# Up projection of an encoder layer: seven block products in place of eight

## The chip, the cores and the metric

The kernel runs on one core of a Trainium2 chip. The metric is the device time of one execution in microseconds (us). Three runs of the kernel before took 3253.85, 3255.36 and 3263.27 us; the median is 3255.36. TensorE is called PE here, VectorE DVE, ScalarE ACT, GpSimd POOL; SP is the engine that issues most DMAs.

## The reference, cut to what matters

One layer of a bidirectional encoder, 2048 tokens of 1024 channels in float32: an input projection, RWKV-7 time mixing beside windowed attention, an output projection with residual, and then a ConvGLU. The change lies in the ConvGLU's up projection, 1024 x 5632:

```python
x = x + jnp.concatenate([y_rwkv, y_attn], axis=-1) @ w_out[l]
x = x + conv_glu(rms_norm(x, g_ffn[l]), w_up[l], conv_w[l], conv_b[l], w_down[l])

def conv_glu(h, w_up, conv_w, conv_b, w_down):
    T = h.shape[1]
    u = h @ w_up                                  # (2048, 1024) @ (1024, 2 * 2816)
    up = jnp.pad(u, ((0, 0), (1, 1), (0, 0)))
    u = sum(up[:, i:i + T] * conv_w[i] for i in range(3)) + conv_b
    g, val = jnp.split(u, 2, axis=-1)
    return (jax.nn.silu(g) * val) @ w_down
```

## The kernel before, in words

The program is a row of stages, each a block of five instruction streams (one per engine) that meet only at semaphores: first, attention, rwkv_project, gates, recurrence, mix, up, down. All tensors lie with 128 channels on the partitions and tokens along the free dimension. A float32 product is made of three matmuls (`product`, L88 to L93): both operands are split into a high part (rounded to fp32r) and a low part (what is left), and high x high, high x low and low x high are summed in PSUM. The high half of a split is a copy on ACT (L2137, L1821 and others), the low half a subtraction on DVE (L2191, L1929).

**Mix** (`mix_block`, L1591) makes x + concat @ w_out in 32 slots, 4 quarters of 512 tokens by 8 tiles of 128 channels, in three PSUM banks in turn. A slot is 24 matmuls on PE, the addition on DVE (L1965), a square on ACT (L1843), a sum on POOL (L1901), and a store to `x2_dram` by SP (L1724). After each quarter PE sums the squares over the channels (L1781), ACT takes the root (L1847) and DVE the reciprocal (L1975), which gives the factor `inv_all` of the norm. While the last quarter runs, mix reads back the first two quarters (L1701), scales them on POOL and DVE (L1890, L1970), splits them, and splits the first two weight tiles; at its end PE already makes two products of the next stage (`up_ahead`).

**Up** (`up_block`, L2011) takes 22 pairs j. A pair is a gate tile and a value tile of 128 output channels each, over all 2048 tokens: 2 tiles x 4 quarters x 8 blocks of depth x 3 matmuls = 192 matmuls. Each quarter has a PSUM bank of its own (8 in all). The split tokens stay in SBUF for the whole stage. ACT copies each finished quarter to `up_raw` (L2148), DVE makes the depthwise convolution from it over 2048 tokens (one tensor_scalar L2210, two scalar_tensor_tensor L2213, L2216), ACT takes the sigmoid (L2154, into the memory of `inv_all`), DVE multiplies twice (L2221, L2226), SP stores (L2065). The weights of the next tiles are loaded into one buffer (L2052) and split. Pairs 1 to 20 are a loop; pair 0 and pair 21 are written out. The order on each engine is the order in which the code is written; no scheduler moves anything.

**Down** (`down_block`, L2256) reads the stored products back, and starts when all engines have left the up stage (`end_phase`, L416).

## Time and profile before

| what | us |
|---|---|
| median of three runs | 3255.36 (3253.85 to 3263.27) |
| profiled execution, span from first to last instruction | 3261.5 |
| mean granted clock of PE over the span | 0.963 |
| PE busy | 2993.0 (92%) |
| DVE busy | 1565.6 (48%) |
| ACT busy | 1039.5 (32%) |
| POOL busy | 770.6 (24%) |
| first matmul of the up projection, last one | 1782.8, 2756.6 |
| first matmul of the down projection | 2775.9 |

The profiled execution is one of its own; its time is known by its span only, which lies between the middle and the slowest of the three runs. The up projection is the longest stage, 974 of 3261 us. A row for a group of instructions gives their number, their busy time, the mean duration of one, and then the idle time of the engine just before them with what ended it. Matmuls overlap in the records: one lasts about 390 ns and the next begins some 227 ns after it began, so the busy share of PE says only that it did not stop. The granted clock is 1.00 at 2.4 GHz and 0.50 at 1.2 GHz.

### The profile page before, as it was taken

How to read it: one execution, taken by the hardware profiler on the slowest of the kernel's cores; microseconds unless marked ns; L12 is line 12 of the kernel's file. 1: busy time of each engine (PE TensorE's matmuls, PEld its weight loads, DVE VectorE, ACT ScalarE, POOL GpSimd, SP SyncE). 2: the span in 40 equal slices, each digit the busy share in tenths (PEclk: the TensorE clock that was granted, in tenths of full speed). 3: DMA queues.
4: the chain of work that ended last, by engine and by line, in shares of the span. 5: the costliest groups of instructions: out<-in, count | busy, mean ns of one | idle time of the engine just before them, and what ended most of it. 6: DMA issues, size and time to landing. Idle time of an engine off the chain costs nothing. (4 is left out here: it accounts for less than half of the span.)

```text
span 3261.5 us, 63594 instructions
## 1 busy us (share of the span) xinstructions
PE 2993.0 (92%) x26436; PEld 2417.1 (74%) x26436; DVE 1565.6 (48%) x2033; ACT 1039.5 (32%) x2012; POOL 770.6 (24%) x874
## 2 busy tenths in 40 slices
PE   7879989997658999996999899999999998999999
PEld 4554578884358999994667788888888886788887
DVE  4556723336665555634446644443444444333333
ACT  4436711114434444433244311111111111222222
POOL 4436700005436777631333300000000000000000
PEclk9998999998869999998999999999999999999999
DMA  3331223224883333224653211111111111631330
GB/s 116 136 91 43 53 78 71 65 52 131 306 248 98 115 118 116 85 91 144 205 168 134 82 49 51 46 38 51 51 51 46 50 51 41 241 100 47 100 100 35
DMA packets 236276, 317.60 MB, mean 97 GB/s; under 512 B 81593, under 2 KB 164025, under 8 KB 233234
## 3 DMA queue, kind: packets, MB, share of 16 engines
q1 hardware_dynamic: 231154, 308.99, 29.6%
q10 hardware_dynamic: 4896, 5.38, 0.5%
q8 instruction: 168, 2.75, 0.4%
q14 instruction: 58, 0.48, 0.1%
HBM read 211.17 MB, written 103.14 MB: 96 GB/s over the span
## 5 line engine op out<-in xcount | busy, mean ns | idle before, releaser
L91 PE MATMUL up_p<-h_hi,up_w_hi 128*128 128x512 f32 x1408 | 550.4, 391 | 10.1 <-DVEq L2187 3.9
L93 PE MATMUL up_p<-h_hi,up_w_lo 128*128 128x512 f32 x1408 | 549.5, 390 | 0.0
L92 PE MATMUL up_p<-h_lo,up_w_hi 128*128 128x512 f32 x1408 | 549.3, 390 | 0.0
L2148 ACT COPY up_raw<-up_p 128x512 f32<-128x512 f32 x176 | 103.3, 588 | 755.9 <-PE up_p L93 749.4
L91 PEld LDWEIGHTS up_p<-h_hi,up_w_hi 128*128 128x128 f32 x1408 | 265.4, 188 | 66.5 <-issue 7.3
L92 PEld LDWEIGHTS up_p<-h_lo,up_w_hi 128*128 128x128 f32 x1408 | 265.4, 189 | 55.6 <-issue 0.2
L93 PEld LDWEIGHTS up_p<-h_hi,up_w_lo 128*128 128x128 f32 x1408 | 265.2, 188 | 55.3
L2210 DVE TENSOR_SCALAR up_con<-up_raw,vecs_sb 128x2048 f32<-128x2048 f32 (+2 forms) x45 | 59.6, 1324 | 500.1 <-ACT up_raw L2148 500.1
L91 PE MATMUL down_p<-down_act_hi,down_w_hi 128*128 128x512 f32 x704 | 275.0, 391 | 18.9 <-DVE down_act_lo L2364 18.9
L92 PE MATMUL down_p<-down_act_lo,down_w_hi 128*128 128x512 f32 x704 | 274.9, 390 | 0.0
L93 PE MATMUL down_p<-down_act_hi,down_w_lo 128*128 128x512 f32 x704 | 274.7, 390 | 0.0
L2361 DVE TENSOR_TENSOR down_w_lo<-down_w,down_w_hi 128x1024 fp32r<-128x1024 f32 x88 | 107.8, 1225 | 308.9 <-ACT down_w_hi L2343 308.9
L2343 ACT CAST down_w_hi<-down_w 128x1024 fp32r<-128x1024 f32 x88 | 92.4, 1050 | 352.1 <-PE down_p L93 336.0
L91 PEld LDWEIGHTS down_p<-down_act_hi,down_w_hi 128*128 128x128 f32 x704 | 132.8, 189 | 47.0 <-issue 19.4
L93 PEld LDWEIGHTS down_p<-down_act_hi,down_w_lo 128*128 128x128 f32 x704 | 132.7, 189 | 27.8
L92 PEld LDWEIGHTS down_p<-down_act_lo,down_w_hi 128*128 128x128 f32 x704 | 132.7, 189 | 27.5
L561 POOL TENSOR_SCALAR attention_prob<-attention_prob,attention_inv 128x384 f32<-128x384 f32 (+1 forms) x96 | 117.1, 1236 | 59.7 <-DVE attention_inv L628 59.7
L1157 POOL TENSOR_TENSOR rec_V<-rec_V,rec_part 128x31 f32<-128x31 f32 (+15 forms) x217 | 123.1, 567 | 17.0
L91 PE MATMUL mix_p_out<-mix_hi,mix_w_hi 128*128 128x512 f32 x256 | 110.9, 433 | 13.7 <-DVE mix_lo L1929 13.7
L1153 POOL TENSOR_TENSOR rec_part<-rec_W,rec_V 128x31 f32<-128x31 f32 (+15 forms) x217 | 118.0, 544 | 22.4 <-issue 6.2
L91 PE MATMUL first_p_proj<-h_hi,first_w_hi 128*128 128x512 f32 x192 | 85.2, 444 | 35.5 <-POOL first_w_lo L357 23.7
L742 ACT COPY rwkv_project_raw_pad<-p_rwkv 128x512 f32<-128x512 f32 x56 | 32.9, 588 | 255.3 <-PE p_rwkv L93 255.3
(255 smaller groups left out, 6421.4 us busy)
## 6 DMA issues: line engine op xcount, KB each, us to landing
rec_inp<-gate_chunks SPq DMA_DIRECT2D x64, 512.0 KB, 3.6
down_act<-act_out SPq DMA_DIRECT2D x88, 256.0 KB, 2.8
up_w<-in_w_up SPq DMA_DIRECT2D x42, 512.0 KB, 4.0
act_out<-up_con SPq DMA_DIRECT2D x21, 1024.0 KB, 4.2
first_w<-in_w_attn SPq DMA_DIRECT2D x24, 512.0 KB, 4.6
rkv_chunks<-rwkv_project_mix SPq DMA_DIRECT2D x12, 1024.0 KB, 6.5
gate_chunks<-gates_out SPq DMA_DIRECT2D x3, 4096.0 KB, 11.7
down_w<-in_w_down SPq DMA_DIRECT2D x22, 512.0 KB, 12.8
```

The costliest lines, as they stand in the source:

```text
L91: pe.matmul(out, w_hi, x_hi, start=start, stop=False)
L92: pe.matmul(out, w_hi, x_lo, start=False, stop=False)
L93: return pe.matmul(out, w_lo, x_hi, start=False, stop=stop)
L561: ops.tensor_scalar(prob[:, i % PB, lo:hi], prob[:, i % PB, lo:hi], inv[:, b % 2, h:h + 1], None, ALU.mult).then_inc(S[name], 1)
L742: nc.scalar.copy(raw[:, b, 1 + n * NT:1 + (n + 1) * NT], p_proj[:, b, n]).then_inc(S[f"copied{b}"], 1)
L1153: ops.tensor_tensor(product, W[:, below, b].unsqueeze(2).to_broadcast([P, n, b + 1]), V[:, b, cols].unsqueeze(1).to_broadcast([P, n, b + 1 ...
L1157: op = ops.tensor_tensor(V[:, below, cols], V[:, below, cols], product, ALU.add)
L2148: nc.scalar.copy(raw[:, half, 1 + n * NT:1 + (n + 1) * NT], p_u[:, half, n]).then_inc(S["copied_" + c], 1)
L2210: nc.vector.tensor_scalar(con[:, half, at], raw[:, half, here], cw(1, half, j), cb(half, j), ALU.mult, ALU.add).then_inc(S["c0" + c], 1)
L2343: nc.scalar.copy(w_hi[:, k % 2], w[:, k]).then_inc(S["w_hi"], 1)
L2361: nc.vector.tensor_tensor(w_lo[:, k % 2], w[:, k], w_hi[:, k % 2].bitcast(F32), ALU.subtract).then_inc(S["w_lo"], 1)
```

## The change

The change works on blocks of half the depth. For one pair and 1024 tokens, let A11 and A12 be the two halves in depth of the gate tile's weights, A21 and A22 those of the value tile, and B the tokens in two halves of the depth by two tiles of 512 tokens. The gate and value results for the two token tiles are four sums C11, C12, C21, C22 of two block products each, eight products in all. By Winograd's form of Strassen's scheme seven are enough, if sums of blocks are multiplied in place of blocks:

- Weights, per pair and pass, on DVE: sum 7 = A11 - A21, sum 6 = A22 - sum 7, sum 4 (into A12) = A12 - sum 6, sum 5 (code name `s1_sum`) = A21 + A22. Seven operands are then split: `a_hi1` .. `a_hi7` on ACT, `a_lo1` .. `a_lo7` on DVE, each 128 x 512.
- Tokens, once per pass: the four sums t1 to t4, and seven operands `b_hi`, `b_lo` of 128 x 4 x 512, of which mix makes the first two.
- Products: PE makes 7, 6, 2, 5, 1 (of the next pair), 3, 4, twelve matmuls each, 84 in place of 96. Some add to a bank that ACT copied in between: product 6 adds to the bank of product 1 after copy s1, product 5 after copy u2, product 3 after copy u4. The results are: c12 = that bank at the end (copied by ACT), c11 = product 2 + s1, c21 = (7 + 4) + u2, and c22 = 7 + u4, taken before product 4 is added. The last three are additions on DVE with an operand in PSUM.

The tokens are done in two passes of 1024, so all 22 pairs run twice, in 44 iterations g, all written out in place of the loop. Here an iteration is called a frame. The weights are loaded in each pass. The convolution of a pass covers 1023 tokens and then 1025; POOL keeps two columns of each pair between the passes (`halo`). The middle tap moves from DVE to ACT. The scaling of the first two quarters in mix moves from POOL and DVE to DVE alone, with the norm's gain in the same instruction, and four loads of 1 MB are issued at one place. The tokens of the second pass are loaded in iteration 1, scaled in iterations 3 to 18, and made into operands in iteration 21, the last of the first pass.

The diff, cut to its core (`done` waits until a semaphore has reached a value; in this order PE, SP, ACT and DVE; `s3_sum` is sum 7, `s2_sum` sum 6, `first_parts` and `second_parts` are the sums and low halves of the tokens, `switch` is iteration 21, `here_now` and `now` are true from iteration 0 on, `load_second` issues the four loads of the second pass):

```diff
-                def body(j, last):
-                    for half, c in enumerate("gv"):
-                        pe.wait_ge(S["w_lo"], j * 2 + half + 1)
-                        for n in range(TN):
-                            pe.wait_ge(S["copied_" + c], j * TN + n + 1)
-                            quarter(half, n)
+                for g in range(G):
+                    x, y = UP_X[g % 2], UP_Y[g % 2]
+                    done(pe, "c21", g - 1)
+                    part(7, g, y, True)
+                    done(pe, "s1", g + 1)
+                    part(6, g, x, False)
+                    if g > 0:
+                        done(pe, "c11", g)
+                        part(2, g, UP_Z, True)
+                    done(pe, "u2", g + 1)
+                    part(5, g, x, False)
+                    if live(g + 1):
+                        done(pe, "c12", g)
+                        part(1, g + 1, UP_X[(g + 1) % 2], True)
+                    done(pe, "u4", g + 1)
+                    part(3, g, x, False)
+                    done(pe, "c22", g + 1)
+                    part(4, g, y, False)
...
+                def part(i, g, to, start):
+                    n = second(g)
+                    done(pe, f"a_lo{i}", g if i <= 2 else g + 1)
+                    a_hi, a_lo, b_hi, b_lo = up_operand(K, i)
+                    for k in range(HALF):
+                        if g % FT == 0 and k % 2 == 0:
+                            done(pe, f"b_lo{i}", filled(i, n, k // 2))
+                        mm = part_product(pe, bank(to), a_hi[:, k], a_lo[:, k], b_hi[:, k], b_lo[:, k],
+                                     start and k == 0, k == HALF - 1)
+                    mm.then_inc(S[f"p{i}"], 1)
...
+                def load_a22(g):
+                    done(sp, "a_lo4", g)
+                    load(g, "22", 1, slice(HALF, KD))
...
+                for g in range(-1, G + 1):
+                    if g >= 0 and live(g + 1):
+                        load_a22(g + 1)
+                    if live(g + 2):
+                        load_a11(g + 2)
+                    if live(g - 1):
+                        store(g - 1)
+                    if live(g + 2):
+                        load_a21(g + 2)
+                        load_a12(g + 2)
+                    if g == 1:
+                        load_second()
...
+                    if here_now:
+                        high4(g)
+                    if switch:
+                        part_high(1, 1)
+                    if live(g - 1):
+                        tap0(1, g - 1)
+                        sigmoid(g - 1)
+                    if live(g + 1):
+                        summed_high(7, g + 1)
+                    if here_now:
+                        u2(g)
...
+                def s2_sum(g):
+                    done(dve, "p6", g)
+                    done(dve, "s3_sum", g + 1)
+                    done(dve, "a22_in", 16 * g)
+                    tt(K.a_sum[6][:, :, :], A["22"], K.a_sum[7][:, :, :], sub).then_inc(S["s2_sum"], 1)
...
+                for g in range(-1, G + 1):
+                    switch = g == LAST
+                    now, ahead = live(g), live(g + 1)
+                    if live(g - 1):
+                        c21(g - 1)
+                    if now:
+                        low(4, g, A["22"])
+                    if switch:
+                        for c in range(2):
+                            part_low(1, 1, c)
+                    if ahead:
+                        s3_sum(g + 1)
+                    if live(g - 1):
+                        taps(1, g - 1)
+                    if ahead:
+                        s2_sum(g + 1)
+                        summed_low(7, g + 1)
+                    if live(g - 1):
+                        gated(g - 1)
+                    if now:
+                        c11(g)
+                    if live(g - 1):
+                        out(g - 1)
+                    if g == -1 or switch:
+                        first_parts(second(g + 1))
+                    if ahead and g >= 0:
+                        low(2, g + 1, A["12"])
+                    if now:
+                        c22(g)
...
+                    if g == -1 or switch:
+                        second_parts(second(g + 1))
```

How the instructions stand on the engines. On DVE, in a steady stretch of the up stage. `up_raw` holds the results before the convolution, `up_con` after it, `inv_all` the sigmoid. Before, from the first pair:

```order
L2210 TENSOR_SCALAR up_con<-up_raw,vecs_sb 128x2048
L2213 SCALAR_TENSOR_TENSOR up_con<-up_raw,vecs_sb,up_con 128x2048
L2216 SCALAR_TENSOR_TENSOR up_con<-up_raw,vecs_sb,up_con 128x2048
L2221 TENSOR_TENSOR up_con<-up_con,inv_all 128x2048
L2226 TENSOR_TENSOR up_con<-up_con 128x2048
```

Now, from c21 of one iteration to c22 of the next; `up_a_sum` and `up_a_lo` are sums and low halves of weight blocks, `inv0` and `inv1` hold the copies u2 and u4:

```order
L2371 TENSOR_TENSOR up_raw<-up_p,inv0 128x512
L2310 TENSOR_TENSOR up_a_lo4<-up_a_raw,up_a_hi4 128x512
L2287 TENSOR_TENSOR up_a_sum7<-up_a_raw 128x512
L2377 SCALAR_TENSOR_TENSOR up_con<-up_raw,vecs_sb,up_con 128x1023
L2380 SCALAR_TENSOR_TENSOR up_con<-up_raw,vecs_sb,up_con 128x1023
L2293 TENSOR_TENSOR up_a_sum6<-up_a_raw,up_a_sum7 128x512
L2310 TENSOR_TENSOR up_a_lo7<-up_a_sum7,up_a_hi7 128x512
L2386 TENSOR_TENSOR up_con<-up_con,up_raw 128x1023
L2360 TENSOR_TENSOR up_raw<-up_p,up_s1 128x512
L2391 TENSOR_TENSOR up_con<-up_con 128x1023
L2310 TENSOR_TENSOR up_a_lo2<-up_a_raw,up_a_hi2 128x512
L2366 TENSOR_TENSOR up_raw<-up_p,inv1 128x512
```

The convolution of the pair before and the splits and sums of the pair after alternate in one queue; the two additions from PSUM on which PE waits (c11, L2360, and c22, L2366) stand behind them.

On ACT, at the start of the up stage. Before (`up_w_hi` is the high half of a whole weight tile):

```order
L2148 COPY up_raw<-up_p 128x512 x2
L2142 ACTIVATE h2_hi<-up_con,vecs_sb 128x512 x8
L2148 COPY up_raw<-up_p 128x512 x2
L2142 ACTIVATE h2_hi<-up_con,vecs_sb 128x512 x8
L2148 COPY up_raw<-up_p 128x512 x4
L2137 CAST up_w_hi<-up_w 128x1024
```

Now, the end of the part ahead of iteration 0 and its first instructions (L2187 is the copy u2, L2192 u4):

```order
L2177 CAST up_b_hi5<-up_stage 128x1024 x2
L2142 CAST up_a_hi1<-up_a_raw 128x512
L2142 CAST up_a_hi3<-up_a_raw 128x512
L2177 CAST up_b_hi3<-up_stage 128x1024 x2
L2177 CAST up_b_hi4<-up_stage 128x1024 x2
L2142 CAST up_a_hi4<-up_a_raw 128x512
L2142 CAST up_a_hi7<-up_a_sum7 128x512
L2187 COPY inv0<-up_p 128x512
L2142 CAST up_a_hi6<-up_a_sum6 128x512
L2142 CAST up_a_hi2<-up_a_raw 128x512
L2192 COPY inv1<-up_p 128x512
```

Copy u2 stands behind the cast of sum 7 of the next pair, which DVE makes after all the token operands of the pass.

On SP, in the first iterations of the up stage. Before:

```order
L2058 DMA up_con<-x2_dram 128x4x512 x2
L2052 DMA up_w<-in_w_up 128x1024 x2
L2065 DMA act_out<-up_con 128x2048
```

Now (`up_stage` is where the second pass's tokens go):

```order
L2053 DMA up_a_raw<-in_w_up 128x512 x9
L2085 DMA act_out<-up_con 128x1023
L2053 DMA up_a_raw<-in_w_up 128x512 x2
L2079 DMA up_stage<-x2_dram 128x4x512 x4
L2053 DMA up_a_raw<-in_w_up 128x512 x2
L2085 DMA act_out<-up_con 128x1023
```

The four loads of 1 MB of tokens stand ahead of the load of A22 for pair 3.

## Rows read from the trace of the kernel before

**Rows 1.** Stage table; columns: window: length, busy us (instructions) per engine, PEclk, DMA, GB/s

```profile
1852.00:2725.00 873.00, 873.00 (x3853) 722.91 (x3852) 376.70 (x200) 168.65 (x221) 0.00 (x0) 1.00 0.13 48
```

**Rows 2.** Waits between 1852 and 2725: who waited for whom, total, times, longest

```profile
ACT up_raw L2148 <- PE up_p L93: 707.2, 161, 4.9
DVE up_con L2210 <- ACT up_raw L2148: 484.1, 40, 14.3
```

**Rows 3.** Groups by line and shape, 1852 to 2725: busy us, mean ns, idle before

```profile
L2191 DVE TENSOR_TENSOR up_w_lo<-up_w,up_w_hi 128x1024 fp32r<-128x1024 f32 x40 | 48.8, 1219 | 0.0
L2226 DVE TENSOR_TENSOR up_con<-up_con 128x2048 f32<-128x2048 f32 x20 | 45.8, 2292 | 0.7
```

**Rows 4.** Timeline of ACT and DVE in mix: start, duration, instruction, idle before

```profile
1736.65 2.17 ACT L1824 CAST mix_hi<-mix_y 128x512 fp32r<-128x512 f32 x4
1738.29 2.48 DVE L1931 TENSOR_TENSOR mix_lo<-mix_y,mix_hi 128x512 fp32r<-128x512 f32 x4
```

**Rows 5.** Timeline of all engines around the start and the end of the up stage

```profile
1779.78 6.15 DVE L1970 TENSOR_TENSOR up_con<-up_con,inv_all 128x512 f32<-128x512 f32 x4 [1.52 <-DMA up_con<-x_dram]
1782.81 0.39 PE L91 MATMUL up_p<-h_hi,up_w_hi 128*128 128x512 f32 x1
1785.85 0.68 DVE L1965 TENSOR_TENSOR mix_x<-mix_p_out,mix_x 128x512 f32<-128x512 f32 x1
1787.28 1.29 POOL L1901 TENSOR_TENSOR mix_total<-mix_total,mix_x_sq 128x512 f32<-128x512 f32 x1 [0.18 <-ACT mix_x_sq L1843]
1788.62 1.12 PE L1781 MATMUL mix_p_total<-mix_total,consts_sb 128*128 128x512 f32 x2 [0.21 <-POOL mix_total L1901]
1792.01 0.67 ACT L1847 ACTIVATE inv_all<-mix_p_total,vecs_sb 128x512 f32<-128x512 f32 x1
1793.67 3.34 DVE L1975 RECIPROCAL inv_all<-inv_all 128x512 f32<-128x512 f32 x1
1799.09 0.77 PE L91 MATMUL up_p<-h_hi,up_w_hi 128*128 128x512 f32 x1 [3.90 <-DVEq L2187]
1834.81 2.35 DVE L2213 SCALAR_TENSOR_TENSOR up_con<-up_raw,vecs_sb,up_con 128x2048 f32<-128x2048 f32 x1
1837.20 2.35 DVE L2216 SCALAR_TENSOR_TENSOR up_con<-up_raw,vecs_sb,up_con 128x2048 f32<-128x2048 f32 x1
2752.09 1.92 ACT L2154 ACTIVATE inv_all<-up_con 128x2048 f32<-128x2048 f32 x1
2756.62 0.39 PE L93 MATMUL up_p<-h_hi,up_w_lo 128*128 128x512 f32 x1
2757.04 0.59 ACT L2148 COPY up_raw<-up_p 128x512 f32<-128x512 f32 x1 [3.04 <-PE up_p L93]
2765.74 0.34 SPq L2083 DMA_DIRECT2D act_out<-up_con  x1
2775.94 0.79 PE L91 MATMUL down_p<-down_act_hi,down_w_hi 128*128 128x512 f32 x1 [18.93 <-DVE down_act_lo L2364]
```

**Rows 6.** DMA issues by line: number, KB each, median us from issue to landing

```profile
down_act<-act_out SPq DMA_DIRECT2D x88, 256.0 KB, 2.8
gate_chunks<-gates_out SPq DMA_DIRECT2D x3, 4096.0 KB, 11.7
first_xt<-in_xT SPq DMA_DIRECT2D x32, 256.0 KB, 5.7
up_con<-x_dram SPq DMA_DIRECT2D x2, 2048.0 KB, 8.0
```

**Rows 7.** PE's clock beside what went before: two windows, and a pause in mix

```profile
1740.00:1783.00 43.00, 43.00 (x189) 35.23 (x188) 26.82 (x27) 13.41 (x19) 16.97 (x12) 1.00 0.57 195
1800.00:1805.00 5.00, 5.00 (x13) 3.86 (x12) 4.08 (x3) 2.95 (x5) 5.00 (x4) 0.51 0.01 3
1563.38 1.12 PE L1745 MATMUL mix_p_mean<-mix_y,consts_sb 128*128 128x512 f32 x2 [1.43 <-POOL mix_y L1883]
...
1567.38 0.39 PE L93 MATMUL mix_p_out<-mix_hi,mix_w_lo 128*128 128x512 f32 x1
```

More of the change, by code:

```diff
@@ new lines, in store @@
+                def store(g):
+                    done(sp, "out", g + 1)
+                    first = 2 * NT - 1 if second(g) else 0
+                    sp.dma_start(K.act_out[g % FT][:, first:first + count(g)], con[:, 1, 0:count(g)]).then_inc(
+                        S["saved"], 16)
+                for g in range(-1, G + 1):
[10 more added lines that the diff above has]
+                        load_second()
@@ L2256, in down_block @@
+        end_phase(nc, S)
 def down_block(nc, K):
```

685 lines of the change are left out of this document (392 added, 293 removed), and 4 rows, old and new, of the table S.

## The prediction, made before the change was run

> **What bounds it now.** I read the table of stages first. In the steady stretch of the up projection (1852 to 2725 us) PE is busy for all 873 us, at granted clock 1.00, with 3853 matmuls [rows 1]: 873 / 3853 = 0.2266 us from one matmul to the next (the 390 ns of a row overlap). VectorE is busy 377 us there, ScalarE 169, GpSimd 0. The list of waits agrees: ScalarE waits 707 us for PE, VectorE 484 us for ScalarE, PE for nobody [rows 2]. So this stage is worth what its matmuls are worth, as long as nothing else takes longer than they do. PE's stretch runs from the first up matmul at 1782.8 to 2757.0: 974.2 us for 4224 matmuls (957.1 at 0.2266) and 17 us of stops.
>
> **What goes.** A pair of gate and value tiles took 2 x 4 x 8 x 3 = 192 matmuls over 2048 tokens. Now it takes 7 x 4 x 3 = 84 over 1024 tokens, in 44 frames (22 pairs, two passes): 3696. That is 528 x 0.2266 = 119.6 us less. A frame is 84 x 0.2266 = 19.03 us if PE sets it.
>
> **VectorE and ScalarE in a frame.** A tensor_tensor of 2048 takes 2.29 us, of 1024 1.22, of 512 0.68 (the addition from PSUM at 1785.85), and four independent ones of 512 in a row take 2.48, so 0.62 each; a scalar_tensor_tensor of 2048 takes 2.35, so 1023 about 1.28 [rows 3 to 5]. A frame holds on VectorE 5 of 0.68 (the sums into raw from PSUM, sum 7, sum 6), 9 of 0.62 (seven low halves, two sums), 4 taps of 1.30 and 2 products of 1.2: 3.4 + 5.6 + 5.2 + 2.4 = 16.6 us, 17.4 in the 16 frames that also scale a row of the second pass. Before it was 377 / 873 = 43% busy; now 87%. ScalarE: 7 casts of 0.54 (four in a row take 2.16), 4 copies of 0.59, 3 activations of 1023 to 1025 at about 1.05 [rows 4, 5]: 9.3 us. Both fit in 19.03, VectorE barely, so its waits decide.
>
> I walk a frame from t=0, when PE starts product 7. Products run 7, 6, 2, 5, next 1, 3, 4 and end at 2.7, 5.4, 8.2, 10.9, 13.6, 16.3, 19.0; a copy from PSUM starts 0.2 later (last matmul at 2756.62, copy at 2757.04 [rows 5]). Product 3 is out at 16.5; ScalarE copies (17.1) and does tap 0 (18.2); VectorE's two gate taps end at 20.8 and low 3 at 21.4, which is 2.4 of the next frame. Then the value sum (3.1), low 4 (3.7), sum 7 (4.4), value taps (7.0), sum 6 (7.7), low 7, gated, c11, out, low 2 (12.0), c22 (12.7), sum 4, low 6, sum 5, low 5 (after 0.6 of waiting for its cast), low 1 (17.1), and taps again at 18.2. PE's nearest deadlines: u2 by 8.2, ready at 6.3 (ScalarE does it only behind tap 0, the sigmoid and cast 7, so behind VectorE's sum 7); u4 by 13.6, ready at 11.7; c22 by 16.3, ready at 12.7. The walk closes with about 1 us to spare, so I take 19.03 for a frame. Low: 19.03, since PE issues no less. High: 0.04 us at each of seven changes of product (the distance of a waiting instruction from its releaser, 1834.81 + 2.35 to 1837.20 [rows 5]), 0.28 x 43 = 12 us. I take 0: the steady stretch held some 160 changes of bank with a wait, and lost nothing.
>
> What the Trainium skill says against it: "VectorE: DVE Perf Modes", in its cycle table and the note on the read-write bubble, has every instruction pay a fixed latency, so that many small tiles cost more than a large one. The rows agree (0.68 for 512 against 2.29 / 4 = 0.57), and my sum holds it.
>
> **The loads.** Four of 256 KB a frame in place of two of 512 KB in 43.5 us, each into its only buffer. The tight one is A22: issued when low 4 is done (3.7), needed by sum 6 at 7.0. A 256 KB load lands 2.8 us after issue in the down stage, 5.7 in the first one [rows 6]. I take 2.8: this stage moves 48 GB/s, and will move some 80 (1.5 MB in 19 us).
>
> **The start.** Mix ends with PE's 32nd tile at 1782.8. Before, VectorE scaled four rows (6.15 us) ahead of the last addition, which came at 1785.85; the last reciprocal ended at 1797.0, and the next stage began 2.1 later (1799.1) [rows 5]. The rows are now scaled earlier, so: addition 1783.1 to 1783.8, square 0.6 (about a copy), GpSimd sum 1.3, matmul 1.1, root 0.7, reciprocal 3.35, end at 1791.2; up starts at 1793.3. The 5 MB that SP now issues together at 1747 delay the x tiles queued behind them, but PE has three banks there; I charge nothing, at most 3 us.
> From there (T=0) VectorE has a long list before PE can run through: sums and low halves of the weights (512 wide) and of the tokens (1024 wide, 1.14 to 1.25 each). Product 7 starts at 8.0, product 6 at 15.8 and ends near 22 (its second token chunk is ready at 19.3), token operands 5, 3 and 4 are done at 27.4, low 4 at 28.0, sum 7 of the next pair at 28.6. Product 5 must wait for all of it: ScalarE's copy u2 stands behind cast 7 of the next pair. So product 5 starts at 29.9. PE idled 8 us; after 3.9 us of idle it ran 13 matmuls at 0.427 apart, granted clock 0.51, that is the 1.2 GHz level, and cost 13 x 0.2 = 2.6 [rows 5, 7]. So 29.9 + 4 x 2.72 + 2.6 = 43.3 for products 5, 1, 3, 4. Their c22 comes at 36.9, in time. Frame 0 ends at 1793.3 + 43 = 1836.3.
>
> **The second pass's tokens.** In iteration 1 SP issues 4 MB for it, and A22 of pair 3 stands behind them in the queue. 2 MB landed in 8.0 us and 4 MB in 11.7 [rows 6], so it lands about 16 into frame 2 in place of 7. Then sum 6, low 7, gated, c11, out, low 2 and c22 (5.7 us) end at 21.8, where product 4 wanted c22 at 16.3: 5.5 us, and 2.6 of slow clock: 8. Ends: 0 (if the loads share the engines) and 12 (at 4 us per MB from the first byte, 16 us for the 4 MB).
>
> **The switch (frame 21).** VectorE gets 22 instructions of 1024 more (8 sums, 14 low halves), 1.14 to 1.25 each: 26 us; ScalarE 14 casts (14.6 us) beside them. All stand in the order ahead of the next c21, and u2 of frame 22 behind that, behind tap 0, sigmoid and cast 7. By the same walk: token operand 4 done at 45.5, c21 46.2, sum 7 47.5, u2 49.5, product 5 of frame 22 from 49.6, then 10.9 + 2.6: frame 22 ends at 62.8 where it would at 38.1. Cost 24.7 (22.1 if the clock stays up).
>
> **The end.** After PE's last matmul VectorE still has gate taps, c21, value taps, gated and out: 8.0 us to the last store, where it was 8.7 (2757.0 to 2765.7), and that store now has twice the bytes (1025 columns against 513). PE stood still for 18.9 us in all [rows 5]. I count 0, at most 2.
>
> **Sum.** From 1782.8: 10.5 + 43.3 + 43 x 19.03 + 8 + 24.7 = 904.8, against 974.2: 69 us less, which is 119.6 of matmuls less 51 of new stops. On this execution 3261.5 becomes 3192 (span). That span lies 6 us above the median of the runs, 3255.4, and 2 us below the slowest, 3263.3; the saving holds for both, so 3255.4 - 69 = 3186.
>
> **Rivals.**
> A. VectorE's ring becomes the bound. From low 4 through the load of A22, sum 6 and all that follows to the next low 4: 0.4 + landing + 16.6 - 0.7 - 2.6 + 0.6 = 14.3 + landing. At 2.8 that is 17.1, below 19.03; at 5.7 [rows 6] it is 20.0, and 43 x 1.0 = 43 more: 3229. For it: VectorE at 87%, one buffer for each block. Against: the queue is nearly empty here.
> B. PE's clock falls (slower than before). PE now changes bank and waits seven times a frame. Rows: a pause of 1.43 us in mix was followed by matmuls that took 0.39 us, the full clock's, and three banks in turn ran at clock 1.00 between 1740 and 1783, while 3.90 us of idle was followed by the 1.2 GHz level [rows 5, 7]. If one pause of that kind came in each frame, 13 slow matmuls would cost 2.6 us x 43 = 112, so 3298; it decides from 69 / 43 = 1.6 us a frame, 8 slow matmuls. Against: the walk has no pause at all in 40 of the 44 frames. The Trainium skill, "TensorE: Matmul & The Clock Gate", section "A second HAM failure mode: psum-queue depth-cycling", describes just this, short idles between groups as the banks cycle; by the stage's own rows there were none.
> C. The long unrolled program starves an engine, where before there was a loop. Against: mix is straight code already, and its matmuls stood 0.227 apart; at the upper end of A it would look the same.
>
> **How the numbers follow.** Forecast 3186, chance 0.68; its own range 3170 (clock stays up three times, 4 MB hidden) to 3210 (changes of product cost 12, later landings 10). A 0.17 (3229, still faster). B 0.08 (3298). 0.07 for a frame near 20.5, at 3245 to 3265. A difference under 0.3%, 10 us, is what a measurement of this kernel can't tell from none. Faster 0.86, same 0.06, slower 0.08. Range 3166 to 3236, which takes in A.
>
> **What would show it.** Right: 3696 matmuls of up_p; frames 19.0 us apart between frame 3 and 20, with VectorE near 87% busy; a stop of some 8 us before product 5 of frame 0, one of some 5 us in frame 2 ahead of product 4 (released by c22, and it by the load of A22), one of 11 us in frame 22. Wrong: PE waits in every frame before product 5 or 4 (A), a granted clock under 1.00 between the three stops (B), waits that the profile puts down to issue (C).

## The result, and the profile after

The changed kernel takes 3207.1 us (median of 4 runs, 3202.9 to 3215.1); the kernel before, run beside it, 3259.1 (4 runs, 3253.9 to 3263.3). The ratio is 0.984, 95% interval 0.983 to 0.986: 52 us less, where I forecast 69 less and 3186. The profiled execution took 3204.8, its span 3202.9.

Totals are a blunt measure here. The stages ahead of the up projection differ from one execution to the next: its first matmul starts at 1782.8 us before and 1770.9 after, and lies within 20 us of range over the kernels below. So I compare the **stage**, from the first to the last matmul into up_p: 973.8 us before [rows 5], 927.0 now, 46.8 less. My sum had 904.8. The miss is 22 us, and it lies inside the stage. Each stage length here comes from the one profiled execution of its kernel. (One run of loads_spread, below, took 10652 us, for a reason that nothing here shows, and is left out of its median.)

Timeline of PE in the changed kernel: the stage's first and last matmul, and those behind a stop of over 0.65 us (start, duration, instruction, idle before it and its releaser):

```profile
1770.91 0.39 PE L99 MATMUL up_p<-up_b_hi,up_a_hi 128*128 128x512 f32 x1
...
1788.46 0.77 PE L99 MATMUL up_p<-up_b_hi,up_a_hi 128*128 128x512 f32 x1 [10.64 <-DVE up_b_lo L2346]
1796.76 0.77 PE L99 MATMUL up_p<-up_b_hi,up_a_hi 128*128 128x512 f32 x1 [3.29 <-DVE up_b_lo L2346]
1800.46 0.50 PE L99 MATMUL up_p<-up_b_hi,up_a_hi 128*128 128x512 f32 x1 [0.80 <-DVE up_b_lo L2346]
1810.87 0.79 PE L99 MATMUL up_p<-up_b_hi,up_a_hi 128*128 128x512 f32 x1 [8.74 <-ACT inv L2187]
1864.11 0.79 PE L99 MATMUL up_p<-up_b_hi,up_a_hi 128*128 128x512 f32 x1 [5.68 <-ACT inv L2192]
2246.79 0.80 PE L99 MATMUL up_p<-up_b_hi,up_a_hi 128*128 128x512 f32 x1 [8.58 <-ACT inv L2192]
2275.22 0.80 PE L99 MATMUL up_p<-up_b_hi,up_a_hi 128*128 128x512 f32 x1 [12.18 <-ACT inv L2187]
2692.43 0.51 PE L99 MATMUL up_p<-up_b_hi,up_a_hi 128*128 128x512 f32 x1 [0.68 <-ACT inv L2192]
2697.90 0.40 PE L101 MATMUL up_p<-up_b_hi,up_a_lo 128*128 128x512 f32 x1
2717.86 0.79 PE L91 MATMUL down_p<-down_act_hi,down_w_hi 128*128 128x512 f32 x1 [19.56 <-DVE down_act_lo L2572]
```

The walk's stops are all here; one is new, at 2246.79, which I had as a part of the next. (The row at 2697.90 is the stage's last matmul, 2717.86 the first of the down stage.) L2187 is the copy u2 ahead of product 5, L2192 the copy u4 ahead of product 3. Counted from the first row, product 7 of frame 0 starts at 17.6 (my 18.5), product 6 at 25.9 (26.3), product 5 at 40.0 (40.4). Frame 2 loses 5.7 us at product 3, the switch 8.6 at product 3 of frame 21 and 12.2 at product 5 of frame 22; the end costs 19.6 before the down stage, against 18.9 [rows 5].

What answers to [rows 1], [rows 7], [rows 2] and [rows 6]. First windows (length, busy us and instructions of PE, PEld, DVE, ACT, POOL, then granted clock, DMA share, GB/s):

```profile
1880.00:2230.00 350.00, 349.87 (x1503) 281.91 (x1503) 303.22 (x376) 172.78 (x253) 6.15 (x18) 1.00 0.22 81
2001.00:2195.00 194.00, 194.00 (x835) 156.32 (x834) 167.67 (x209) 95.61 (x140) 4.05 (x10) 1.00 0.22 82
...
1864.00:1868.00 4.00, 3.89 (x9) 3.09 (x10) 3.87 (x6) 0.06 (x1) 0.00 (x0) 0.51 0.23 95
```

The same 194 us of the kernel before:

```profile
2001.00:2195.00 194.00, 194.00 (x858) 160.64 (x857) 80.95 (x44) 38.65 (x50) 0.00 (x0) 1.00 0.13 46
```

Then VectorE's wait for block A22 ahead of frame 2 (total, times, longest), the weight loads of the stage (number, KB, us to landing), and of the groups between 1880 and 2230 (busy, mean ns) one of the three of matmuls:

```profile
DVE up_a_sum L2293 <- DMA up_a_raw<-in_w_up: 10.1, 1, 10.1
```

```profile
up_a_raw<-in_w_up SPq DMA_DIRECT2D x172, 256.0 KB, 2.7
```

```profile
L100 PE MATMUL up_p<-up_b_lo,up_a_hi 128*128 128x512 f32 x501 | 199.5, 398 | 0.0
```

VectorE is busy 303.2 / 350 = 87%, the clock is 1.00, the loads land in 2.7 us, and PE has no gap to speak of. But 194 us hold 835 matmuls, where 194 us of the kernel before hold 858 (a window also counts the one or two that reach into it, so the distances are 0.2328 and 0.2266 us, the latter as in [rows 1]). The distance between ScalarE's sigmoids, one a frame, is 19.56 to 19.57 us in 34 frames, where I had 19.03. That is 0.53 x 43 = 23 us, about the whole miss, and no view of waits shows it: PE counts as busy, since its matmuls overlap. (The rest nearly cancels: the last frame has no product 1, so 43 whole frames were 2.7 us too many, and the stops came to some 2 us more than the sum had.) It shows in the mean duration, too (392 to 398 ns, where the kernel before's took 389), and best in the distances between starts. In ns, product 1 and then product 3 of one frame of the changed kernel:

```
229 233 236 224 231 236 228 233 230 227 227 226 | 237 232 237 231 232 237 231 232 237 231 232
```

Product 1 goes over to the 226 and 227 of the kernel before; every other product repeats 237, 231, 232. What sets product 1 apart is where its operands lie. The weight operands of products 2 to 7 start at byte 96 of 128 in each partition (the allocator puts them behind the padded raw, con and halo tiles), those of product 1, all token operands, and both sides of the kernel before at byte 64. (These places are read from the tiles as the allocator lays them; the trace does not hold them.)

### The profile page after: what moved, and what is told of

Its sections match the earlier page's. It is cut to its first block and busy times, and to the rows that moved or that the text cites. A ratio compares the mean times of both kernels' runs of the same rounds, so it can differ in the third digit from the quotient of the medians.

```text
span 3202.9 us, 64182 instructions
## 1 busy us (share of the span) xinstructions
PE 2899.0 (91%) x25908; PEld 2316.9 (72%) x25908; DVE 1894.2 (59%) x2727; ACT 1282.9 (40%) x2386; POOL 747.2 (23%) x895
## 5 line engine op out<-in xcount | busy, mean ns | idle before, releaser
L99 PE MATMUL up_p<-up_b_hi,up_a_hi 128*128 128x512 f32 x1232 | 492.1, 399 | 50.9 <-ACT inv L2187 20.9
L100 PE MATMUL up_p<-up_b_lo,up_a_hi 128*128 128x512 f32 x1232 | 494.7, 402 | 0.0
L101 PE MATMUL up_p<-up_b_hi,up_a_lo 128*128 128x512 f32 x1232 | 487.0, 395 | 0.0
L99 PEld LDWEIGHTS up_p<-up_b_hi,up_a_hi 128*128 128x128 f32 x1232 | 234.2, 190 | 115.3 <-ACT inv L2187 22.4
L91 PE MATMUL down_p<-down_act_hi,down_w_hi 128*128 128x512 f32 x704 | 274.7, 390 | 19.6 <-DVE down_act_lo L2572 19.6
L101 PEld LDWEIGHTS up_p<-up_b_hi,up_a_lo 128*128 128x128 f32 x1232 | 234.0, 190 | 56.0
L100 PEld LDWEIGHTS up_p<-up_b_lo,up_a_hi 128*128 128x128 f32 x1232 | 234.4, 190 | 53.6 <-issue 0.2
L2142 ACT CAST up_a_hi<-up_a_sum 128x512 fp32r<-128x512 f32 x132 | 81.4, 616 | 216.1 <-DVE up_a_sum L2302 138.7
L2212 ACT ACTIVATE up_con<-up_raw,vecs_sb 128x1023 f32<-128x1023 f32 (+1 forms) x88 | 109.7, 1246 | 123.3 <-DVE up_raw L2371 96.1
L2377 DVE SCALAR_TENSOR_TENSOR up_con<-up_raw,vecs_sb,up_con 128x1023 f32<-128x1023 f32 (+1 forms) x88 | 113.1, 1286 | 70.9 <-ACT up_con L2212 70.9
L2310 DVE TENSOR_TENSOR up_a_lo<-up_a_raw,up_a_hi 128x512 fp32r<-128x512 f32 x174 | 119.2, 686 | 12.8 <-ACT up_a_hi L2142 12.8
```

The costliest lines, as they stand in the source:

```text
L91: pe.matmul(out, w_hi, x_hi, start=start, stop=False)
L99: pe.matmul(out, w_hi, x_hi, start=start, stop=False, skip_group_check=True)
L100: pe.matmul(out, w_hi, x_lo, start=False, stop=False, skip_group_check=True)
L101: return pe.matmul(out, w_lo, x_hi, start=False, stop=stop, skip_group_check=True)
L2212: nc.scalar.activation(con[:, half, 0:count(g)], raw[:, half, cols(g)], ACT.Identity, scale=cw(1, half, g), bias=cb(half, g)).then_inc(S[f ...
L2310: tt(K.a_lo[i][:, :, :], of, f32(K.a_hi[i][:, :, :]), sub).then_inc(S[f"a_lo{i}"], 1)
```

## The experiments

The durations in this table are of the stage in each one's profiled execution; "frame" is the mean distance of sigmoids over frames 9 to 18. Differences of 2 us between two stages rest on one execution each.

| kernel | stage us | frame us | whole us, median (runs) | ratio to before, 95% |
|---|---|---|---|---|
| before | 973.8 | | 3259 to 3265 | |
| changed | 927.0 | 19.57 | 3207.1 (4) | 0.983 to 0.986 |
| a_aligned | 913.4 | 19.21 | 3202.4 (5) | 0.981 to 0.984 |
| b_shifted | 923.3 | 19.43 | 3208.3 (4) | 0.983 to 0.986 |
| before_shifted | 996.5 | | 3275.9 (4) | 1.003 to 1.007 |
| loads_spread | 912.8 | 19.21 | 3198.5 (3) | 0.978 to 0.983 |
| a_at_64 | 914.8 | 19.28 | 3204.6 (4) | 0.979 to 0.983 |
| both_at_0 | 915.0 | 19.26 | 3202.5 (1) | |
| both_at_96 | 913.7 | 19.23 | 3211.2 (1) | |
| loads_behind | 906.7 | 19.30 | 3192.7 (4) | 0.976 to 0.979 |
| sum_on_pool | 893.9 | 19.04 | 3181.9 (4) | 0.973 to 0.978 |
| start_order | 902.3 | 19.27 | 3195.2 (1) | |
| switch_on_pool | 908.9 | 19.35 | 3195.2 (1) | |
| best | 888.4 | 19.04 | 3176.7 (5) | 0.971 to 0.974 |

### Where the operands lie

**a_aligned**, after the halo tile:

```diff
+        up.enter_context(hold("up_pad", [P, 8], F32))
         for i in (3, 4, 5, 6, 7, 2):
             hold_a(up, i)
```

> The changed kernel with 32 bytes of padding ahead of the weight operands of products 2 to 7. In the changed kernel these operands begin at byte addresses that are 32 above a multiple of 64; those of product 1, and every weight operand of the kernel before, begin at a multiple of 64. Nothing else is touched: no instruction, wait or order. In the trace of the changed kernel a frame took 19.565 us in place of 19.03, without a stop of PE, and only product 1 ran at 0.2266 us from matmul to matmul. Theory 1 (a weight operand that is not at a multiple of 64 bytes slows each of its matmuls by 6.7 ns): the window 1900 to 2200 shows 0.2266 us per matmul (1324 matmuls), the 43 frames take 19.03 us, 3207 becomes 3184 us, ratio 0.977 to before. Rival 2 (seven changes of product and their waits in each frame cost the 0.53 us): no change, 0.2326 us per matmul, 3207 us. Rival 3 (VectorE, ScalarE and the DMAs at 87%, 48% and 22% take SBUF cycles from PE): no change, or less than 3 us.

**b_shifted**, the same line ahead of the token operands:

```diff
+        up.enter_context(hold("up_pad", [P, 8], F32))
         for i in (3, 4, 5, 6, 7):
             hold_b(up, i)
```

> The same 32 bytes of padding put ahead of the token operands of products 3 to 7 instead, so that these (the moving side of the matmuls) begin 32 above a multiple of 64, while all weight operands are at a multiple of 64; the token operands of products 1 and 2 stay aligned. Theory 1a (only the side that is loaded as weights matters): 0.2266 us per matmul, frame 19.03, 3184 us, as with the weights aligned alone. Rival 1b (either side matters): the slow spacing stays in products 3 to 7, frame about 19.4, 3200 us. Rival 2 (changes of product): 3207 us.

**before_shifted**, the kernel before:

```diff
-    with (hold("up_w_hi", [P, 2, KD, P], F32R) as K.up_hi, hold("h2_hi", later, F32R) as K.h_hi,
+    with (hold("pad4", [P, 8], F32), hold("up_w_hi", [P, 2, KD, P], F32R) as K.up_hi,
+          hold("pad5", [P, 24], F32), hold("h2_hi", later, F32R) as K.h_hi,
```

(and the same about both up_w_lo tiles; up_w_hi then starts at byte 96 and up_w_lo at 32. The two paddings together also move h2, the tokens of three of the four quarters, by 128 bytes.)

> The kernel before, its loop and its work unchanged, with its weight operands of the up projection (both tiles' high and low halves) moved so that they begin 32 above a multiple of 64. Theory 1: its steady stretch goes from 0.2266 to 0.2333 us per matmul (3853 matmuls in 873 us become about 3740), so 4224 x 6.7 ns = 28 us more: 3259 becomes 3287 us, ratio 1.0085. Rivals 2 and 3 (the cause is in the order of products or in the load on the other engines): 3259, no change, since neither differs from the kernel before.

The window from 2001 to 2195 in a_aligned and b_shifted, and the stretch of [rows 1] in before_shifted:

```profile
2001.00:2195.00 194.00, 194.00 (x850) 159.18 (x849) 171.63 (x213) 93.06 (x140) 2.22 (x10) 1.00 0.24 82
```

```profile
2001.00:2195.00 194.00, 194.00 (x839) 157.16 (x838) 169.58 (x211) 94.21 (x141) 4.24 (x10) 1.00 0.24 81
```

```profile
1852.00:2725.00 873.00, 873.00 (x3776) 708.34 (x3775) 365.57 (x194) 163.59 (x215) 0.00 (x0) 1.00 0.13 46
```

before_shifted shows that the place of tiles alone costs time: the old loop, the old work, and 3776 matmuls where there were 3853, 0.2312 us each, the stage 22.7 us longer (28 expected), the whole 0.3 to 0.7% slower. That excludes changes of product and busy neighbours as its cause. But my rule was wrong. With the weights at byte 0 (a_aligned) matmuls stood 226, 229, 232 ns apart, better than 237 and still not 226.7, so its usual frame of 19.20 us is just the sum of its distances; and with tokens at 96 against weights at 0 (b_shifted) all of it came back (230, 237, 231). So it is not the weight side alone. I formed another: what counts is whether both sides lie at the same place within 128 bytes.

**a_at_64**, **both_at_0** and **both_at_96** differ in the two paddings (in floats, ahead of the token and the weight operands): 0 and 24, 16 and 24, 8 and 24.

> The changed kernel with 96 bytes of padding ahead of the weight operands of products 2 to 7: they begin 64 above a multiple of 128, as the token operands do, and as the weight operands of the kernel before and of product 1 do. Measured so far by steady spacing: weights and tokens both at 64 (of 128) 0.2266 us per matmul; weights at 0, tokens at 64: 0.229; weights at 96, tokens at 64: 0.2338; weights at 0, tokens at 96: 0.233. Theory 1 (the two sides must stand at the same place within 128 bytes; difference decides) and theory 1' (64 is the good place by itself): all products at 0.2266, frame 19.03; the up projection from its first to its last matmul takes 904 us in place of 927 (913 with the weights at 0), the whole 3184 us. Rival (what is left over 0.2266 in the run with weights at 0 is the changes of product or the neighbours' traffic): frame 19.2, 913 us.

> Token operands of products 3 to 7 and weight operands of products 2 to 7 all moved to a multiple of 128 bytes (product 1 has both at 64, product 2 weights at 0 and tokens at 64). Theory 1 (the difference decides): products 3 to 7 at 0.2266, only product 2 at 0.229; frame 19.06. Theory 1' (each side's own place decides, 64 is the good one): products 2 to 7 at 0.229 or more, frame 19.2 or more.

> Token operands of products 3 to 7 moved by 32 bytes, so that they begin at 96 of 128 as the weight operands of products 2 to 7 do in the changed kernel. Theory 1 (the difference decides): products 3 to 7 at 0.2266, product 2 (weights at 96, tokens at 64) stays at 0.2338; frame 19.11. Theory 1' (each side must start at a multiple of 64): nothing gets better, products 2 to 7 at 0.233 or more, frame 19.56 or more.

Distances between starts in ns, each kernel in the same steady stretch:

```
a_at_64     any product                        227 227 226 227 227 226 227 227 226
both_at_0   products 3 to 7 (0 and 0)          227 227 226 227 227 226 227 227 226
both_at_0   product 2 (weights 0, tokens 64)   234 233 233 234 233 233 234 233 233
both_at_96  products 3 to 7 (96 and 96)        227 227 226 227 227 226 227 227 226
both_at_96  product 2 (weights 96, tokens 64)  234 235 232 235 232 235 231 235 232
```

The difference decides: at 96 and 96, the place that looked bad, products 3 to 7 settle at 226.7, while product 2, whose sides differ, stays slow in the same frame. Weights at 64 are not needed for it. (Behind a stop or a change of place some ten matmuls stand 224 to 236 ns apart before they settle; so product 3 of both_at_0 and both_at_96, behind product 1, still has a few of these.)

What a difference costs looks irregular within 128 bytes: weights 0 and tokens 64 cost 2.2 ns in a_aligned and 6.7 in both_at_0. Counted within 256 bytes, which I had not done, it is not: those are weights 128 and tokens 192 in the one, 0 and 192 in the other. In these kernels (before_shifted apart, where the high and low weights differ) weights less tokens is 0 wherever matmuls stand 226.7 apart (192/192, 0/0, 224/224), -64 where they stand 229, and -96, -192 or 32 where they stand 233 to 234. A difference of 128 alone occurs nowhere, so whether "the same byte of 128" is enough, or it must be the same of 256, no run shows.

Yet the frames did not come to 19.03. Aligned, a_at_64 has frames of 19.11 to 19.67 us, 19.28 in the mean of frames 9 to 18, and its stage is no shorter than a_aligned's. In six of these ten frames product 5 starts 0.1 to 0.5 us late, and a few matmuls behind it stand 228 to 236 ns apart. Most of it is too short to be listed as a stop; the largest is, as 0.3 us put down to u2 (L2187). PE was not alone at the bound. The waits of VectorE in a_at_64, 2001 to 2195, ten frames:

```profile
DVE up_a_lo L2310 <- ACT up_a_hi L2142: 10.5, 20, 0.7
DVE up_con L2377 <- ACT up_con L2212: 7.7, 21, 0.6
DVE up_a_sum L2293 <- DMA up_a_raw<-in_w_up: 0.2, 1, 0.2
```

These are two waits a frame for a cast and two for ScalarE's tap 0. The changed kernel has the same ones (10.5 and 11.3 us), so the list alone does not say what binds. The way from sum 5 to the next taps does, here from the timelines of both engines in one frame:

```profile
2092.39 0.68 DVE L2302 TENSOR_TENSOR up_a_sum<-up_a_raw 128x512 f32<-128x512 f32 x1
2093.16 0.62 ACT L2142 CAST up_a_hi<-up_a_sum 128x512 fp32r<-128x512 f32 x1 [5.33 <-DVE up_a_sum L2302]
2093.68 0.58 ACT L2182 COPY up_s<-up_p 128x512 f32<-128x512 f32 x1
2094.16 0.62 ACT L2142 CAST up_a_hi<-up_a_raw 128x512 fp32r<-128x512 f32 x1
2094.68 0.59 ACT L2198 COPY up_raw<-up_p 128x512 f32<-128x512 f32 x1
2095.45 1.25 ACT L2212 ACTIVATE up_con<-up_raw,vecs_sb 128x1023 f32<-128x1023 f32 x1 [0.17 <-ACT up_raw L2198]
2096.73 1.28 DVE L2377 SCALAR_TENSOR_TENSOR up_con<-up_raw,vecs_sb,up_con 128x1023 f32<-128x1023 f32 x1 [0.56 <-ACT up_con L2212]
```

A ring of VectorE and ScalarE: sum 5, its cast, copy s1, the cast for product 1, copy c12, tap 0, and then taps 1 and 2 on VectorE and its list up to the next sum 5. From the end of sum 5 to those taps it takes 3.65 us in each of the ten frames, none of it waiting for PE, and the rest 15.5 to 16.0: 19.11 to 19.67 in all. Between the switch and frame 31, where PE has no stop and its frames take 19.04, the sigmoids still come 19.20 us apart in the mean. In the changed kernel the same way takes 4.1 us, since c12 waits for PE there, so the ring lay hidden under the wide matmuls. Why the rest varies between 15.5 and 16.0 is open.

### The loads of the second pass

**loads_spread** (on a_aligned) and **loads_behind** (on a_at_64): one 1 MB load an iteration, at the end of SP's list, or right behind A22.

```diff
                     if g >= 0 and live(g + 1):
                         load_a22(g + 1)
+                    if 1 <= g <= 4:                              # loads_behind
+                        load_second((g - 1) // 2, (g - 1) % 2)
...
                         load_a12(g + 2)
-                    if g == 1:
-                        load_second()
+                    if 1 <= g <= 4:                              # loads_spread
+                        load_second((g - 1) // 2, (g - 1) % 2)
```

> The kernel with aligned weight operands, and the four 1 MB loads of the second pass's tokens issued one an iteration (1 to 4) in place of all four in iteration 1. In the changed kernel VectorE waited 10.1 us for block A22 of pair 3, which stood behind them, and PE stopped 5.7 us in frame 2. My step in the prediction (8 us: 5.5 of stop and 2.6 of the low clock level): the wait and the stop go, and 8 us with them against the kernel with aligned weights: 3176 us. Rival (the stop is the late finish of the first frame's list on VectorE, and the load only fills the same time): a stop of about 5 us stays in frame 2 or 3, 3184 us.

> The kernel with weight operands at 64, and the second pass's four 1 MB loads issued one an iteration (1 to 4), each right behind the load of block A22 in place of ahead of it. When they were spread so that each stood just ahead of A22, VectorE waited 2.5 to 2.9 us for A22 in each of four frames, these took 21.1 us, and nothing was gained. Theory (only what stands in the queue ahead of A22 costs, since A11, A21 and A12 have most of a frame): no stop in frames 1 to 5, all at 19.03 us; 8 us less than with the weights at 64 alone (stop of 6 us and the low clock level): up projection 896 us, the whole 3176. Rival (any 1 MB load beside a frame's four blocks costs 2 us, since the engines are shared): frames 1 to 5 at 20 to 21 us, and no gain, 904 us.

SP's queue in loads_spread, in one of the frames (start, duration, issue; where issues are merged, the duration runs over all of them):

```profile
1895.22 7.19 SPq L2053 DMA_DIRECT2D up_a_raw<-in_w_up  x2
1902.51 0.38 SPq L2076 DMA_DIRECT2D up_stage<-x_dram  x1
1903.28 0.93 SPq L2053 DMA_DIRECT2D up_a_raw<-in_w_up  x2
```

and VectorE there:

```profile
1909.16 0.69 DVE L2290 TENSOR_TENSOR up_a_sum<-up_a_raw,up_a_sum 128x512 f32<-128x512 f32 x1 [2.55 <-DMA up_a_raw<-in_w_up]
```

The end of SP's list is a bad place: A12's buffer comes free only at the end of a frame, so the 1 MB (L2076) goes out 0.8 us ahead of the next A22 (the first of the two behind it). The stop of frame 2 went, and four frames of 21.1 to 22.1 us took its place: stage 912.8 against 913.4, nothing. Behind A22 the loads are nearly free: sigmoids 29.8, 19.5 and 19.5 us apart in a_at_64 are 19.1, 20.6 and 19.1 apart now, and the stage goes from 914.8 to 906.7, 8.1 us less. The theory's step holds, but for the one frame of 20.6; its 896 does not, since it started from 904 and not from 914.8. Frames 1 to 19 alone give back 9.8 us; frames 20 to 42 lose 2.0 of it again, for which no cause is shown.

### The ring, the start and the switch

**sum_on_pool** (on loads_behind) moves one instruction a frame; the loads of A21 and A22 wait for it:

```diff
-                        s1_sum(g + 1)              # on VectorE, ahead of low 5
...
+                def s1_sum(g):                     # on GpSimd
+                    if live(g):
+                        done(pool, "p5", g)
+                        done(pool, "a21_in", 16 * g)
+                        done(pool, "a22_in", 16 * g)
+                        nc.gpsimd.tensor_tensor(K.a_sum[5][:, :, :], A["21"], A["22"], ALU.add).then_inc(
+                            S["s1_sum"], 1)
```

> The kernel with aligned operands and the loads behind A22, and the sum of blocks A21 + A22 (512 wide, once a frame) made by the idle GpSimd in place of VectorE. Measured in the two aligned kernels: every product at 0.2266 us per matmul, and still frames of 19.11 to 19.67 us, with PE 0.1 to 0.3 us late at product 5 (released by ScalarE's copy u2); VectorE has 0.74 us of waiting for ScalarE's cast of that sum in each frame. Theory (VectorE's and ScalarE's ring, sum, cast, copies, tap 0, taps, is as long as the frame, so it sets what is over 19.1): 0.6 us of work and 0.7 of waiting leave the ring, all frames come to 19.11; the up projection 907 - 40 x 0.2 = 899 us, the whole 3185. Rival (the ring is closed by the load of A22, from low 4 to sum 6): frames stay at 19.1 to 19.6, 907 us. Second rival (GpSimd takes SBUF cycles from VectorE beside it): VectorE's 512-wide instructions go from 0.69 to over 0.8 us in places, and the frames get longer.

```profile
2001.00:2195.00 194.00, 194.00 (x858) 160.63 (x857) 176.38 (x204) 96.75 (x142) 23.02 (x21) 1.00 0.25 82
```

858 matmuls, the kernel before's own number, and every frame away from the switch and the two ends 19.03 to 19.05. The stage is 12.8 us shorter (8 expected): 8.5 in frames 1 to 19 and 23 to 42, 4.2 in frames 20 to 22 around the switch. VectorE's waits for casts are gone, and its wait for tap 0 grew to as much as 1.2 us, as that now hangs on PE through c12: the ring is open. The second rival is half right: VectorE is held up, but the frames do not get longer. Timeline of VectorE and of GpSimd in one frame:

```profile
2079.98 1.78 DVE L2316 TENSOR_TENSOR up_a_lo<-up_a_raw,up_a_hi 128x512 fp32r<-128x512 f32 x1
```

```profile
2079.31 1.89 POOL L2271 TENSOR_TENSOR up_a_sum<-up_a_raw 128x512 f32<-128x512 f32 x1 [12.59 <-PE up_p L101]
```

The low half that meets GpSimd's sum takes 1.78 us in place of 0.69. It ends 0.6 us after the sum does, as if it had stood until the sum was done.

**start_order** (on loads_behind), frame 0 alone: ScalarE's u2 behind the casts of token operand 4, u4 behind high 4; VectorE's c22 behind low 4.

```diff
                         part_high(4, second(g + 1))
+                    if g == -1:
+                        u2(0)
...
                         high4(g)
+                    if g == 0:
+                        u4(0)
```

> The kernel with the loads behind A22; for frame 0 alone, ScalarE's copies u2 and u4 stand ahead of the cast of sum 7 of the next pair, and VectorE's c22 right behind low 4. In the prediction, product 5 of frame 0 waits for all of VectorE's list, because u2 stands behind that cast. Theory: the stop of 8.7 us at product 5 goes, since product 6 ends at 12 to 13 us after the first product's start and the low half of token operand 5 is there then; VectorE's own list sets PE a little later instead (u2 of frame 1 behind the taps), which gives 3 to 4 us back: 5 us less, the up projection 902 us. Rival (VectorE's backlog is all that counts): the stop moves into frame 1 whole, 907 us.

PE's stops at product 5 of frames 0 and 1:

```profile
1818.54 0.50 PE L99 MATMUL up_p<-up_b_hi,up_a_hi 128*128 128x512 f32 x1 [0.80 <-ACT inv L2184]
1843.18 0.79 PE L99 MATMUL up_p<-up_b_hi,up_a_hi 128*128 128x512 f32 x1 [5.17 <-ACT inv L2184]
```

The stop fell from 8.75 us to 0.80, and one of 5.17 came in frame 1: 902.3 against 906.7, 4.4 less, as the theory had it. So about half of the stop was the order, and the other half is VectorE's list.

**switch_on_pool** (on loads_behind):

```diff
+                def token_sums():                  # GpSimd, frame 21; ahead of it on VectorE
+                    for c in range(2):
+                        tt(K.b_sum[7][:, chunk(c)], stage[:, 3, chunk(c)], stage[:, 1, chunk(c)], ALU.subtract)
+                        tt(K.b_sum[6][:, chunk(c)], K.b_sum[7][:, chunk(c)], stage[:, 0, chunk(c)], ALU.add)
...
```

> The kernel with the loads behind A22; in frame 21 the eight sums of token chunks for the second pass (1024 wide, 10 us on VectorE) are made by GpSimd, and ScalarE's u4 of that frame stands ahead of the casts of those sums. In frames 21 and 22 PE stops 9.0 and 12.3 us and starts at the low clock level three times; predicted cost of this place 24.7 us, as 26 us more of VectorE's work. Theory (PE waits for VectorE's sum of work there): 10 us less of it, the stops come to about 12 us, the up projection 907 - 9 = 898 us. Rival (the order is what costs, and the token operands are wanted as soon as GpSimd makes them, which takes 2.4 us for each in place of 1.2): the first stop goes, the second grows by as much, 905 to 910 us.

Neither: the first stop did not go, though 908.9 lies in the rival's range. PE's stops in frames 21 and 22 sum to 26.2 us where loads_behind has 22.6, the stage is 2.2 us longer, and for a reason I had not priced. VectorE (first fence) beside GpSimd (second):

```profile
2218.06 2.88 DVE L2331 TENSOR_TENSOR up_a_lo<-up_a_raw,up_a_hi 128x512 fp32r<-128x512 f32 x1
2220.86 0.68 DVE L2392 TENSOR_TENSOR up_raw<-up_p,inv 128x512 f32<-128x512 f32 x1
...
2223.66 6.64 DVE L2367 TENSOR_TENSOR up_b_lo<-up_stage,up_b_hi 128x1024 fp32r<-128x1024 f32 x2
2230.22 2.82 DVE L2308 TENSOR_TENSOR up_a_sum<-up_a_raw 128x512 f32<-128x512 f32 x1
```

```profile
2217.18 3.22 POOL L2271 TENSOR_TENSOR up_b_sum<-up_stage 128x1024 f32<-128x1024 f32 x1 [2.81 <-PE up_p L101]
2220.54 2.65 POOL L2275 TENSOR_TENSOR up_b_sum<-up_b_sum,up_stage 128x1024 f32<-128x1024 f32 x1
2223.14 2.79 POOL L2271 TENSOR_TENSOR up_b_sum<-up_stage 128x1024 f32<-128x1024 f32 x1
```

For 24 us each of VectorE's instructions with two SBUF inputs takes about as long as one of GpSimd's: 2.88 in place of 0.69, and 6.64 for two in place of 2.35. The two engines look to take turns. The one that reads PSUM (up_p) kept its 0.68. The Trainium skill, "SBUF — State Buffer", section "Who interferes with whom", says that a VectorE instruction with two SBUF inputs contends with a GpSimd instruction that reads SBUF, and calls the shared pair of ports an exclusive lock. The trace agrees (0.69 us became 2.88). So eight sums that took 10 us of VectorE's time held it up for 16 us on GpSimd, counted over its eight slow instructions between 2218 and 2243.

**best**: sum_on_pool, with the order of start_order for frames 0 and 22, and

```diff
+                    if switch:
+                        c21(g)                     # VectorE, ahead of low halves of token operand 5
```

> What helped so far, together: aligned operands, loads behind A22, the sum A21 + A22 on GpSimd, and the order of the first frame; the same order at the switch too (ScalarE's u2 and u4 of frame 22 ahead of the casts for pair 23, VectorE's c21 of frame 21 ahead of the low halves of token operand 5). Theory (the gains add, since each removes a different stop): up projection 894 us with the sum on GpSimd, less 4.4 for the first frame, less about 3 at the switch (c22 of frame 22 still waits for VectorE's list, which comes to the same end): 887 us, the whole 3175 us, ratio 0.973 to before and 0.990 to the changed kernel. Rival (VectorE is behind at both places, and an earlier u2 is given back whole at the next wait): 894 us, 3182, ratio 0.975.

888.4 us, within 1.4 of the 887 of the theory, and 3176.7 for the whole: 0.971 to 0.974 of the kernel before, 30 us under the changed kernel. Against sum_on_pool frames 0 to 5 give 4.9 us (4.4 expected) and the order at the switch 0.8, where about 3 were expected. Of the switch these are left in PE's timeline:

```profile
2235.17 0.80 PE L99 MATMUL up_p<-up_b_hi,up_a_hi 128*128 128x512 f32 x1 [9.29 <-ACT inv L2190]
2268.92 0.80 PE L99 MATMUL up_p<-up_b_hi,up_a_hi 128*128 128x512 f32 x1 [9.20 <-DVE up_raw L2375]
```

L2375 is c22: the stop at product 5 of frame 22 became one at product 4, behind VectorE's list. What is left at the switch, the moved stop suggests, is VectorE's work.

## Why the prediction was right, and where it was not

- **What goes** (119.6 us, 3696 matmuls): right. The page of the profile has 3 x 1232 matmuls of up_p.
- **The start**: right within 1 us at each of three products. Its cause was half the matter: start_order takes the stop at product 5 away by moving the copies and c22, but 5.2 us of it come back in frame 1.
- **The second pass's tokens** (8 us: 5.5 of stop, 2.6 of the low clock level): VectorE waited 10.1 us for A22, PE stopped 5.7 us and ran eight matmuls at the low clock level, 1.8 more: 7.5. It came at product 3, through u4, which stands behind the cast of sum 6, and not at product 4 through c22 as I had it. loads_behind gives back 8.1.
- **The switch** (24.7): 8.6 + 12.2 of stops, 1.6 and 2.7 of the low clock level: 25.1. I had one stop, in frame 22; the first, in frame 21, came from u4 standing behind the casts of the token sums. So the sum was right and the places were not. That VectorE's work sets the sum, wherever PE stops, fits best, which moved the second stop without ending it; no run takes that work away.
- **The end** (0): 19.6 us against 18.9.
- **VectorE's share** (87%): right in part by luck. Most frames of that window also scale a row, for which my sum had 17.4 us, 91% of 19.03; measured are 16.9 us of 19.57.
- **The frame** (19.03, upper bound 19.31): the step that failed, mis-sized by 0.53 us a frame, 23 us, which is twice my upper bound. In its place the runs showed two causes, one under the other. The first sets the changed kernel's frame. I took 0.2266 us from matmul to matmul from the kernel before and never asked what sets it ("PE issues no less"); it holds only for operands that lie alike, and here they stood 0.2328 apart. Mending the placement gives 0.29 us a frame (927.0 to 914.8) until the second binds; with the second mended alone a frame would, by the sum, still take 84 x 0.2328, which no run tries. My bound priced changes of product, which cost at most 0.01 us a frame (19.04 in sum_on_pool). Second, "the walk closes with about 1 us to spare" was wrong. It let VectorE go from sum 5 to the next taps with one wait of 0.6 and two low halves, 1.8 us, and let tap 0 wait for PE alone; but s1, the cast for product 1, c12 and tap 0 stand behind the cast of sum 5 on ScalarE, 3.65 us. So the ring takes 19.11 at least, over the 19.04 of PE; opened, the stage goes from 906.7 to 893.9.
- **Rival A** did not come in the changed kernel: PE has no stop in its steady frames. A ring of VectorE is the bound once placement is mended, but not A's: A22's landing was not its limit (0.2 us of waiting in ten frames of a_at_64), ScalarE's casts and copies were. In loads_spread, with A22 2 to 3 us later, frames took 21.1 to 22.1, which is A's mechanism at work.
- **Rival B** (clock): the clock was 1.00 but for 5 to 13 matmuls at the 1.2 GHz level behind each stop of over 3 us. **Rival C**: none of PE's idle time was put down to issue in the frames; of ScalarE's it was 9.3 us between 1880 and 2230, with PE never stopped by it.

The result lies in the forecast's own range (3170 to 3210), near its upper end: the sign and the places were right, and one term of 43 equal parts was 0.53 us a part too small. That it still lies there is in part luck: the 10 and 12 us that the range held for later landings and changes of product were spent on neither.

## What to carry to other kernels

When a change repacks tiles, write down where both operands of each hot matmul start within 256 bytes and keep them alike, with padding where needed; count matmuls in equal windows, since no list of waits shows a wider spacing. A walk through a ring must follow the order on both engines: what stands behind a cast on ScalarE turned 1.8 us into 3.65, and a ring of 18 us into one of 19.1 and more. Put a large load behind the small one that is wanted next, and compare stages, not totals, where the program varies by more than the effect.

## What the runs showed of the hardware

- Matmuls of 512 columns with a weight load each stood 226.7 ns apart when both operands started at the same byte of 256 (192 and 192, 0 and 0, 224 and 224), 229 with weights 64 bytes below tokens, and 233 to 234 with weights 96 or 192 below or 32 above (231 in before_shifted, with mixed distances). The mechanism is not shown. Distances of 128 alone and of 16 bytes were not tried.
- VectorE's instructions with two SBUF inputs were held up beside GpSimd's sums: 0.69 us became 1.78 beside one sum and 2.88 beside a row of them, while one that reads PSUM kept its 0.68.
- A stop of 5.7 us left PE at the 1.2 GHz level (granted clock 0.51) for eight matmuls 0.427 us apart, which cost 1.8 us; one of 12.2 us cost 2.7.
